# Down projections of nine pairs of F tiles as Strassen products, with x kept in DRAM

## What is computed

```python
def swiglu(x, w_gate, w_up, w_down):
    return (jax.nn.silu(x @ w_gate) * (x @ w_up)) @ w_down

x = x + 0.5 * swiglu(rmsnorm(x, n1), f1g, f1u, f1d)
...
x = x + m @ w_out
x = x + 0.5 * swiglu(rmsnorm(x, n3), f2g, f2u, f2d)
```

## Time and profile before

| | us |
|---|---|
| runs | 2576.39, 2578.94, 2579.69; median 2578.94 |
| the profiled execution | 2580.29 |
| its span, first to last instruction | 2578.5 |
| TensorE matmuls busy | 2539.3 (98%) |
| VectorE, ScalarE, GpSimd busy | 1620.6, 1111.3, 44.6 |

### The profile page before, as it was taken

How to read it: one execution, slowest core, us unless ns; L and a number is a source line. 1 busy time by engine, 2 the same in 40 slices (tenths; PEclk the granted TensorE clock), 3 DMA queues, 4 the chain that set the end, 5 groups by cost and what they waited for, 6 DMA issues and landing times.

```text
span 2578.5 us, 50206 instructions
## 1 busy us (share of the span) xinstructions
PE 2539.3 (98%) x19145; PEld 2500.5 (97%) x19145; DVE 1620.6 (63%) x2861; ACT 1111.3 (43%) x1927; POOL 44.6 (2%) x50
## 2 busy tenths in 40 slices
PE   8999999999998999999999999999999999999998
PEld 7999999999998999999999999999999999999997
DVE  6766555655588677667577765443585566565656
ACT  5322232232266776666566654311533222222324
POOL 0000000000020000000000000000200000000000
PEclk9999999999999999999999999999999999999999
DMA  3111111111131212111321225323111111111112
GB/s 120 50 49 49 49 49 49 49 49 49 52 115 34 77 63 78 66 58 59 103 96 65 98 74 197 143 99 123 34 42 50 49 49 49 49 49 50 53 52 75
DMA packets 51162, 177.89 MB, mean 69 GB/s; under 512 B 5505, under 2 KB 9985, under 8 KB 50561
## 3 DMA queue, kind: packets, MB, share of 16 engines
q1 hardware_dynamic: 51072, 176.66, 19.7%
HBM read 146.41 MB, written 30.23 MB: 69 GB/s over the span
## 4 chain that ended last, share of the span: by engine, by line
PE 90%; DVE 5%; ACT 2%; issue 1%; DMA 0%; SPq 0%; POOL 0%; DVEq 0%; ACTq 0%; POOLq 0%
PE banks L138 28%; PE banks L139 28%; PE banks L140 28%; PE banks L1560 1%; PE banks L1341 1%; PE banks L1351 1%; DVE mix_blk_lo L435 1%; PE banks L1353 1%; DVE f_hid_lo L658 1%; PE banks L1383 1%; PE banks L1357 1%; DVE f_gt L806 1%; DVE f_snap L798 1%; ACT f_hid_hi L652 1%; PE banks L1326 0%
## 5 line engine op out<-in xcount | busy, mean ns | idle before, releaser
L138 PE MATMUL banks<-f_blk_hi,f_u_hi 128*128 128x258 f32 x2496 | 707.7, 284 | 4.5 <-DVE f_blk_lo L435 4.5
L139 PE MATMUL banks<-f_blk_lo,f_u_hi 128*128 128x258 f32 x2496 | 706.8, 283 | 0.0
L140 PE MATMUL banks<-f_blk_hi,f_u_lo 128*128 128x258 f32 x2496 | 705.9, 283 | 0.0
L138 PE MATMUL banks<-mix_blk_hi,mix_u_hi 128*128 128x258 f32 x1808 | 525.1, 290 | 1.8 <-DVE mix_blk_lo L435 1.2
L139 PE MATMUL banks<-mix_blk_lo,mix_u_hi 128*128 128x258 f32 x1808 | 511.4, 283 | 0.0
L140 PE MATMUL banks<-mix_blk_hi,mix_u_lo 128*128 128x258 f32 x1808 | 510.1, 282 | 0.0
L138 PEld LDWEIGHTS banks<-f_blk_hi,f_u_hi 128*128 128x128 f32 x2496 | 472.3, 189 | 6.4 <-issue 3.2
L139 PEld LDWEIGHTS banks<-f_blk_lo,f_u_hi 128*128 128x128 f32 x2496 | 472.1, 189 | 0.1
L140 PEld LDWEIGHTS banks<-f_blk_hi,f_u_lo 128*128 128x128 f32 x2496 | 472.1, 189 | 0.0
L138 PEld LDWEIGHTS banks<-mix_blk_hi,mix_u_hi 128*128 128x128 f32 x1808 | 342.1, 189 | 6.2 <-DVE mix_blk_lo L435 1.8
L138 PE MATMUL banks<-f_hid_hi,f_u_hi 128*128 128x344 f32 x1056 | 341.9, 324 | 3.8 <-DVE f_hid_lo L658 3.3
(11 more groups left out here) (257 smaller groups left out, 3630.5 us busy)
## 6 DMA issues: line engine op xcount, KB each, us to landing
raw<-w_slabs SPq DMA_DIRECT2D x220, 512.0 KB, 3.2
sg_kept<-sgt SPq DMA_DIRECT2D x8, 1032.0 KB, 5.6
sgs<-sg_kept SPq DMA_DIRECT2D x16, 516.0 KB, 4.5
x<-x_t SPq DMA_DIRECT2D x8, 516.0 KB, 8.3
x_kept<-x SPq DMA_DIRECT2D x1, 4128.0 KB, 12.1
oa_kept<-sq SPq DMA_DIRECT2D x8, 516.0 KB, 2.9
ob_kept<-z SPq DMA_DIRECT2D x8, 516.0 KB, 2.7
h_f<-oa_kept SPq DMA_DIRECT2D x4, 1032.0 KB, 6.1
```

The source lines that it names most:

```text
L138: pe.matmul(out, wh, xh, start=start, stop=False, skip_group_check=chained)
L139: pe.matmul(out, wh, xl, start=False, stop=False, skip_group_check=chained)
L140: return pe.matmul(out, wl, xh, start=False, stop=stop, skip_group_check=chained)
```

## The change

A pair's down projection becomes a block product as well, for the pairs 1 to 9: F tiles two, the row tiles of D in even and odd ones, tokens in two halves. The seven products of pair i - 1 run in the group of pair i, between its gate and its up products (`down_pairs`). Each is taken for four blocks of 128 columns (c and q, two by two) with 2 quarters x 3 matmuls of 258 columns. The hidden tiles are written (with the factor 0.5) into seven blocks that lie where x lay in SBUF; VectorE forms four differences of them (`hid_tees`) and both engines split them (`hid_high`, `hid_low`). The seven units of a down need four sums as well, and the ring has 7 slots instead of 6.

The four results of a column block, each 128 x 516, are formed by ScalarE and VectorE in four buffers `part[kind]` of two halves (q): ScalarE copies the bank pair after products 0, 2, 3 and 6 (kinds 0, 2, 1, 3), VectorE adds the bank pair after products 1, 4 and 5 to the copy (kinds 0, 1, 2; kind 3 is the copy alone). GpSimd then issues an accumulating transfer that adds the buffer to x in DRAM (`x_sum`). ScalarE waits on `x_added[kind]` before it writes such a buffer again. x is written to DRAM in four transfers of 1 MB behind pair 0's down and read back in two, for the columns up to 344 and the rest, ahead of pair 10's plain down, which comes last. The loops of SyncE and GpSimd are unrolled; some semaphores are shared and some regions of SBUF moved. The order of the weight slabs in DRAM follows the new order.

```diff
+FIRST_SLABS = 6
 FIRST_PRODUCTS = 8
-FFN_PRODUCTS = 14
+LAST_DOWN = 3
+DOWN_PAIRS = ((3, 2), (1, 0))
+ADDED = 16 + 64 * (PAIRS - 2)
...
+def chain_wait(pe, s, i, c, j, q):
+    if j == 0:
+        if c == 1:
+            pe.wait_ge(s.mixed, mixes(i, down_mix(0, 2, q)))
+        elif q == 1:
+            pe.wait_ge(s.mixed, mixes(i, 1))
+    if j == 1:
+        if c == 1:
+            pe.wait_ge(s.snap, snaps(i, down_snap(0, 3, q)))
+        elif q == 0:
+            pe.wait_ge(s.mixed, mixes(i, 3))
+        else:
+            pe.wait_ge(s.silu, i * 4 + 4)
+    if j == 2:
+        pe.wait_ge(s.snap, snaps(i, down_snap(c, 0, q)))
+    if j == 3:
+        pe.wait_ge(s.mixed, mixes(i, down_mix(c, 0, q)))
+    if j == 4:
+        pe.wait_ge(s.snap, snaps(i, down_snap(c, 1, q)))
+    if j == 5:
+        pe.wait_ge(s.snap, snaps(i, down_snap(c, 2, q)))
+    if j == 6:
+        pe.wait_ge(s.mixed, mixes(i, down_mix(c, 1, q)))
...
+    def down_pairs(i):
+        for c in range(2):
+            for j in range(7):
+                if c == 0:
+                    pe.wait_ge(s.unit_lo, units(i, unit_number(i, 1, j)))
+                    pe.wait_ge(s.norm.block_lo, hid_count(i - 1, j))
+                for q in range(2):
+                    chain_wait(pe, s, i, c, j, q)
+                    pair = DOWN_PAIRS[c ^ (j in (1, 3, 5))][q]
+                    for g in range(2):
+                        cols = slice(g * QW, (g + 1) * QW)
+                        last = three(pe, k.bank[2 * pair + g][:, 0:QW], ffn_weight(s, j, 2 * c + q),
+                                     (s.hb_r[:, 2 * j, cols], s.hb_r[:, 2 * j + 1, cols]),
+                                     j in (0, 1, 3), True, chained=True)
+                    last.then_inc(s.prod, 1)
...
-    def group(i, last=False):
-        for up in range(2):
-            for j in range(7):
-                product7(i, up, j)
-        down(i, last)
+    def group(i):
+        for j in range(7):
+            product7(i, 0, j)
+        if not is_one(i):
+            down_pairs(i)
+        for j in range(7):
+            product7(i, 1, j)
     first_pair()
-    down(0)
-    with pe.Fori(1, PAIRS - 1) as i:
+    down(True)
+    group(1)
+    with pe.Fori(2, PAIRS - 1) as i:
         group(i)
-    group(PAIRS - 1, last=True)
+    group(PAIRS - 1)
+    down(False)
...
+def hid_high(act, k, s, i, j):
+    if j in HID_IN:
+        act.wait_ge(s.hidden, i * 4 + {B11: 1, B22: 2, B21: 3}[j])
+    else:
+        act.wait_ge(s.norm.tees, hid_tee(i, {T1: 1, T3: 2, T2: 3, T4: 4}[j]))
+    act.activation(s.hb_r[:, 2 * j, :], hid_f(s, j), ACT.Copy).then_inc(s.norm.block_hi, 1)
+def hid_low(dve, k, s, i, j):
+    dve.wait_ge(s.norm.block_hi, hid_count(i, j))
+    if j not in HID_IN:
+        dve.wait_ge(s.norm.tees, hid_tee(i, 4))
+    dve.tensor_tensor(s.hb_r[:, 2 * j + 1, :], hid_f(s, j),
+                      s.hb_r[:, 2 * j, :].bitcast(F32),
+                      ALU.subtract).then_inc(s.norm.block_lo, 1)
...
+def hid_tees(dve, k, s, i):
+    n = s.norm
+    t1, t2, t3, t4 = (hid_f(s, j) for j in (T1, T2, T3, T4))
+    dve.wait_ge(n.block_lo, hid_count(i, B21))
+    dve.wait_ge(s.hidden, i * 4 + 4)
+    dve.tensor_tensor(t1, t3, t1, ALU.subtract).then_inc(n.tees, 1)
+    dve.tensor_tensor(t3, t3, t2, ALU.subtract).then_inc(n.tees, 1)
+    dve.wait_ge(n.tees, hid_tee(i, 2))
+    dve.tensor_tensor(t2, t2, t1, ALU.subtract).then_inc(n.tees, 1)
+    dve.wait_ge(n.tees, hid_tee(i, 3))
+    dve.tensor_tensor(t4, t4, t2, ALU.subtract).then_inc(n.tees, 1)
...
+    def down_part(i, c, n, q):
+        kind = (0, 2, 1, 3)[n]
+        act.wait_ge(s.prod, prods(i, down_prod(c, (0, 2, 3, 6)[n], q)))
+        act.wait_ge(k.x_added[kind], s.added_base + (i * 64 + (32 * c - 112)))
+        pair = DOWN_PAIRS[c ^ (n == 2)][q]
+        act.activation(halves(s.part[kind][:, q, :]), both(k, pair), ACT.Copy).then_inc(s.snap, 1)
...
+    def group(i, last=False):
+        unit_high(act, k, s, i, 0, 6)
+        snap(i, 0, 0)
+        hid_high(act, k, s, i - 1, T2)
+        hid_high(act, k, s, i - 1, T3)
+        hid_high(act, k, s, i - 1, T1)
+        hid_high(act, k, s, i - 1, T4)
+        unit_high(act, k, s, i, 1, 0)
+        silu(i, 0)
+        unit_high(act, k, s, i, 1, 1)
+        snap(i, 0, 1)
+        unit_high(act, k, s, i, 1, 2)
+        snap(i, 0, 2)
+        unit_high(act, k, s, i, 1, 3)
+        silu(i, 1)
+        unit_high(act, k, s, i, 1, 4)
+        unit_high(act, k, s, i, 1, 5)
+        silu(i, 2)
+        silu(i, 3)
+        for c in range(2):
+            down_part(i, c, 0, 0)
+            down_part(i, c, 0, 1)
+            if c == 0:
+                unit_high(act, k, s, i, 1, 6)
+            else:
+                unit_high(act, k, s, i, 2, 0)
+                unit_high(act, k, s, i, 2, 1)
+            for n in (1, 2):
+                for q in range(2):
+                    down_part(i, c, n, q)
+            if c == 1:
+                for j in (2, 3, 4, 5):
+                    unit_high(act, k, s, i, 2, j)
+            for q in range(2):
+                down_part(i, c, 3, q)
+        unit_high(act, k, s, i, 2, 6)
+        behind_up(i, last)
...
+    def down_part(i, c, n, q):
+        part = halves(s.part[n][:, q, :])
+        dve.wait_ge(s.prod, prods(i, down_prod(c, (1, 4, 5)[n], q)))
+        dve.wait_ge(s.snap, snaps(i, down_snap(c, (0, 2, 1)[n], q)))
+        pair = DOWN_PAIRS[c ^ (n != 1)][q]
+        dve.tensor_tensor(part, both(k, pair), part, ALU.add).then_inc(s.mixed, 1)
...
     def group(i, last=False):
+        hid_tees(dve, k, s, i - 1)
+        unit_low(dve, k, s, i, 0, 6)
+        hid_low(dve, k, s, i - 1, T2)
+        hid_low(dve, k, s, i - 1, T3)
         mix(i, 0, 0)
+        hid_low(dve, k, s, i - 1, T1)
+        hid_low(dve, k, s, i - 1, T4)
         unit_sums(dve, k, s, i, 1, (0, 1, 2, 3))
+        for j in range(4):
+            unit_low(dve, k, s, i, 1, j)
         mix(i, 0, 1)
+        unit_low(dve, k, s, i, 1, 4)
         mix(i, 0, 2)
+        unit_low(dve, k, s, i, 1, 5)
+        for c in range(2):
+            down_part(i, c, 0, 0)
+            if c == 0:
+                unit_low(dve, k, s, i, 1, 6)
+            down_part(i, c, 0, 1)
+            if c == 0:
+                unit_sums(dve, k, s, i, 2, (0, 1, 2))
+            else:
+                unit_low(dve, k, s, i, 2, 0)
+                unit_low(dve, k, s, i, 2, 1)
+            for n in (1, 2):
+                for q in range(2):
+                    down_part(i, c, n, q)
+            if c == 0:
+                unit_sums(dve, k, s, i, 2, (3,))
+        for j in range(2, 7):
+            unit_low(dve, k, s, i, 2, j)
+        behind_up(i, last)
...
+def ffn_gpsimd(pool, k, s):
+    pool.wait_ge(s.down_used, NT * KT)
+    for kind in range(4):
+        rows = slice(2 * kind * P, 2 * (kind + 1) * P)
+        pool.dma_start(s.x_sum[rows, :].rearrange("(m p) t -> p m t", p=P), s.x[:, 2 * kind:2 * kind + 2, :])\
+            .then_inc(k.x_added[kind], 16)
+    for kind in range(4):
+        pool.wait_ge(k.x_added[kind], s.added_base + 16)
+    def group(i):
+        for c in range(2):
+            for kind in range(4):
+                e, h = ((0, 0), (1, 1), (1, 0), (0, 1))[kind]
+                for q in range(2):
+                    if kind < 3:
+                        pool.wait_ge(s.mixed, mixes(i, down_mix(c, kind, q)))
+                    else:
+                        pool.wait_ge(s.snap, snaps(i, down_snap(c, 3, q)))
+                    m = 2 * (2 * c + q) + e
+                    pool.dma_start(s.x_sum[m * P:(m + 1) * P, half(h)], s.part[kind][:, q, :], accum_op=ALU.add)\
+                        .then_inc(k.x_added[kind], 16)
+    for i in range(2, PAIRS):
+        group(i)
...
+    def row(i, n, c):
+        sp.wait_ge(s.unit_lo, units(i, 7 * (n - 1) + (2, 6)[c]))
+        if c == 0:
+            sp.wait_ge(s.sums, summed(i, 4 * n))
+        load(i * 6 + (s.first - 2 + 2 * n + c), c)
+    for i in range(2, PAIRS):
+        for n in range(3):
+            for c in range(2):
+                row(i, n, c)
+    for c in range(2):
+        row(PAIRS, 0, c)
+    for kind in range(4):
+        sp.wait_ge(k.x_added[kind], s.added_base + ADDED)
+    for t, cols in enumerate((slice(0, TG), slice(TG, T))):
+        sp.dma_start(s.x[:, :, cols], s.x_sum.rearrange("(m p) t -> p m t", p=P)[:, :, cols])\
+            .then_inc(k.x_back[t], 16)
```

More of the change, by code:

```diff
@@ L538, in down @@
                 if first and n in (0, 2):
                     pe.wait_ge(s.silu if n == 0 else s.hidden, 4)
+                if not first and n == 0:
+                    pe.wait_ge(s.hidden, i * 4 + 4)
                 for f in range(2):
-                    done = three(pe, k.bank[DOWN_BANKS[n % 4]][:, 0:TG], ffn_weight(s, base + 2 * (m // 4) + f, m % 4),
+                    slot, b = (2 + 2 * (m // 4) + f, m % 4) if first else (2 * (m % 2) + f, m // 2)
+                    last = three(pe, k.bank[DOWN_BANKS[n % 4]][:, 0:TG], ffn_weight(s, slot, b),
```

(80 more changed lines are left out.)

516 lines of the change are left out of this document (302 added, 214 removed).

## The result

The changed kernel takes 2686.64 us (median of 4 runs, 2676.61 to 2687.92) against 2579.32 for the kernel before (2576.39 to 2580.07): a ratio of 1.041 (1.0383 to 1.0436), 107 us slower. The forecast was 2532 us. The profiled execution took 2686.25 us, its span is 2684.4 us.

What follows compares the result with a forecast made beforehand. TensorE, busy 98%, was taken to bound the kernel. From the profiled 2580.3 us, 54.0 came off for matmuls and the old wait, 7.2 were added for late transfers: 2533.5, less 1.4 for the median, 2532 us; range 2521 to 2572.

Steps and rivals of the forecast that it cites:

- Matmuls and the wait before down: Down projection, 18 pairs: shorter matmul time saves 47.9 us, the vanished wait for the hidden low half 6.1 us more.
- rival A: All accumulating transfers land in time, no new wait: 2525 us; chance 0.58 together with the forecast's own range.
- VectorE and ScalarE at nothing: Both engines' added work per group, 45.5 and 33.3 us of 60.5, fills neither and is costed at nothing.
- The margins of 0.7 us: Tightest bank waits in the down keep about one VectorE instruction of slack; a slip costs a pair up to 0.7 us.
- Rival B: Partial give-back of 1.3 to 2.7 us a pair by late landings or VectorE's queue: 2548 to 2574 us, chance 0.22.
- C's way through a GpSimd locked out by VectorE: Each of four issues waits up to 0.7 us while VectorE runs mixes: 3.2 us late, 2583 us, chance 0.03.
- The accumulating transfers: GpSimd's adds to x in DRAM: kind 2 lands 0.4 us late for block 1's copy, +7.2 us over 18 pairs.
- 7.2 + 4d + L: Kind 2's landing after the down's start; issue time d 1.08 us, landing L 4.0 us: 15.5, due at 15.1.
- Throughput is no limit: Accumulating transfers: 4.2 MB per 60.5 us, 70 GB/s, against over 400 GB/s in places and engines 15% busy.
- If GpSimd keeps pace: Condition on the down's transfers: GpSimd's last kind 2 issue and its landing together have 5.8 us.
- Rival C: GpSimd and accumulation set the pace, kind 2 landing over 3.0 us late: slower, 2583 to 2599 us, chance 0.14.
- x out and back: Dump of x after pair 0 and reload before pair 10's down are hidden, 4 us to spare, at no cost.

Runs made afterwards that it cites:

- the plain writes: Changed kernel with GpSimd's 16 transfers a pair overwriting x in DRAM instead of adding to it, so sums are lacking: 2528.09 us, ratio 0.9805.
- half of the additions: Changed kernel without column block 0's eight transfers a pair, so its rows lack the sums: 2539.15 us, ratio 0.9852.
- the merged transfers: Changed kernel with both halves q in one accumulating transfer, eight of 516 KB a pair instead of sixteen of 258 KB: 2739.2 us, ratio 1.0628.
- the DRAM to DRAM additions: Changed kernel with SyncE writing buffers to scratch DRAM and GpSimd adding from there to x, pair 9 adding directly: 2701.89 us, ratio 1.0478.

## Why the prediction was wrong

**Matmuls and the wait before down: right.** Their terms are -54.0 us, so 2525 without a transfer's cost (rival A); the plain writes measured 2528.1 (49.3 us less than the kernel before, run beside it), and a pair 60.58 for 60.5.

**VectorE and ScalarE at nothing: right.** The margins of 0.7 us held; no wait came from them in the plain writes. Rival B's way through VectorE's order, and C's way through a GpSimd locked out by VectorE, have no support: beside the same VectorE work a plain issue takes 0.54 us and an adding one 0.85 to 1.2 (mean 0.98), and held issues start 0.3 us after a landing. The Trainium skill's trap ("SBUF — State Buffer", SBUF: two separate sides), a GpSimd-issued transfer that stands still beside VectorE's two-port modes, did not show: the plain issues took 0.54 us throughout.

**The accumulating transfers: the step that failed.** Its two sizes were near: d = 0.98 in the mean for 1.08, and L = 4.1 nearly alone for 4.0; in the crowd of its own kind L was 6.2 for the last of kind 2 in the down above. By 7.2 + 4d + L with d = 0.98 and L = 6.2 one gets 17.3, 2.2 us late, not 5.9; and that sum counts the last d twice, since a landing is timed from the start of its issue (7.2 + 3d + L gives 16.3, and 14.4 with the forecast's own sizes, in time). What failed were the two sentences around them.
- "Throughput is no limit". It was worked out in bytes and over a whole pair. The additions come within the 20.2 us of the down, and each takes 1.91 us of all 16 engines, 2.7 times a write: 30.6 us of work. The bytes a second of the earlier trace rows were those of plain transfers with other shapes, and said nothing of this one. The 15% of the earlier trace rows was the load without these transfers.
- "If GpSimd keeps pace". It does not: the fourth issue waits for the landing of the second, the sixth for that of the fourth. The forecast had the last issue of kind 2 start at 10.4 (7.2 + 3d). Its mix was done at 9.6, but it started at 14.8, 4.4 us later than forecast; with its 6.2 us it landed at 21.0, where the forecast had 15.5.

**The clock: a term that was missing.** Rival C priced a late landing by its lateness alone. The starts at the 18 waits are 5.6 us apart in the mean, so 5.5 late: by that alone 18 x 5.5 = 99 us, 2624. The measured kernel pays 7.70 a pair in the first FFN and 8.01 in the second, some 2.3 more, since the clock is at 1.2 GHz at each wait and stays there for some us of work behind it (1.9 us in the down above). The rows of the runs, by the time between two starts: 3 to 4.7 us stand beside 3.41 or 6.83 us of half clock, 5.6 beside 6.83 (once 3.41), 8 beside 10.24 or 6.83, 12 beside 13.65, 2.2 to 2.7 beside 3.41 or none, and less beside none.

**x out and back "hidden, with 4 us to spare": wrong.** At the end of the first FFN of the change 3.1 and 4.2 us pass between starts at 751.5 and 772.8, each with 3.41 us of half clock. At the first of them ScalarE waits for an addition that lands at 750.1, before it may split a hidden tile. The second waits for x: the last addition landed at 754.6, so that the reload began 17.7 us into the up products and not 6, and its two loads, 1.4 and 2.8 MB, took 6.2 and 14.2 us where "2 x 9.0 us at most" was taken from loads of 2.1 MB each. With plain writes the reload did begin at 5.8. With half of the additions one wait of 5.5 us is left. Most of the 17 us above is of this kind.

**The rivals.** C is the mechanism that came, with its place and its point of decision (over 3.0 us late), at a chance of 0.14; its price, 2583 to 2599, left out the held issues, the clock and the ends. The ledger of the loss over plain writes: 99 us for the waits (18 x 5.5), 42 for the rest of a pair's loss, mainly the clock (18 x 2.3), 17 outside the pairs; the last two have no term in the forecast. Of the signs of being wrong that the prediction named, a group over 63 us and a wait at the reload of x came; the clock digit of the page, a third, stayed at 9 although the clock fell.

What stays open: which resource holds an issue behind two or three times 128 rows. Rows, not bytes and not the number of transfers, fit all three sizes, and the DRAM to DRAM additions too, of which up to four with 96 rows each were on their way. But three plain writes of 1 MB with 256 rows each were issued at once, with the fourth held, so an adding row seems to count for more than a plain one; and the merged transfer has another access pattern besides its 256 rows. Open too is how the change's own loss divides between the held issues and the busy engines.

## What to carry to other kernels

Price a kind of transfer that the trace does not have by what it occupies, not by bytes: an addition in DRAM took 2.7 times the engine time of a write here, and GpSimd kept no more than three of them on their way. Set that work against the stretch in which it is issued, not the whole loop, and ask what becomes of the weight loads beside it. Waits of TensorE of 4 us and more cost a stretch at half clock on top here, so a late landing was dearer than its lateness.
